# Where TensorE's operands are reordered: VectorE writes them plainly, TensorE reads every fourth column

## The reference

```
x = layer_norm(ALPHA * x + mix, ln1_g, ln1_b)            # (256, 1024)
logits = x @ router_w + router_b;  top 4 of 32 experts, softmax of the four
per expert:  gu   = x[tokens] @ w_gu[e] + b_gu[e]        # 1024 -> 2048
             gate = min(gu[:, :1024], 7);  up = clip(gu[:, 1024:], -7, 7)
             act  = gate * sigmoid(1.702 * gate) * (up + 1)
             y    = act @ w_dn[e] + b_dn[e]              # 1024 -> 1024
out = layer_norm(ALPHA * x + weighted sum of the y's, ln2_g, ln2_b)
```

## Time and profile before

| | us |
|---|---|
| median of three runs | 1175.49 |
| the profiled execution's own time | 1174.48 |
| its span (first to last instruction) | 1172.5 |
| TensorE busy | 1071.5 (91%) |
| VectorE busy | 291.3 (25%) |
| ScalarE busy | 146.0 (12%) |
| DMA queue of the weights | 87.8% of 16 engines' span |

### The profile page before, as it was taken

How to read it: one execution, slowest core, us unless ns; L and a number is a source line. 1 busy time by engine, 2 the same in 40 slices (tenths; PEclk the granted TensorE clock), 3 DMA queues, 4 the chain that set the end, 5 groups by cost and what they waited for, 6 DMA issues and landing times.

```text
span 1172.5 us, 14722 instructions
## 1 busy us (share of the span) xinstructions
PE 1071.5 (91%) x5364; PEld 458.4 (39%) x5365; DVE 291.3 (25%) x770; ACT 146.0 (12%) x313; POOL 29.2 (2%) x54
## 2 busy tenths in 40 slices
PE   7999897888999999998989889999999999999983
PEld 6778544332334333323233323333344333333321
DVE  2354645121212212121212212122212212121114
ACT  2044501010011110000000100001011000000000
POOL 3000400000000000000000000000000000000000
PEclk9999998998999999999999989999999999999997
DMA  9623439764999999999999998999999999999993
GB/s 311 247 110 72 168 137 386 301 241 191 405 427 425 428 427 425 428 427 425 427 427 425 427 427 338 427 425 427 427 425 427 427 426 426 427 426 426 427 420 134
DMA packets 48980, 426.32 MB, mean 364 GB/s; under 512 B 5034, under 2 KB 8923, under 8 KB 16155
## 3 DMA queue, kind: packets, MB, share of 16 engines
q1 hardware_dynamic: 48378, 425.37, 87.8%
q10 hardware_dynamic: 576, 0.61, 0.2%
HBM read 424.91 MB, written 1.05 MB: 363 GB/s over the span
## 4 chain that ended last, share of the span: by engine, by line
PE 62%; DMA 28%; DVE 4%; SPq 3%; issue 2%; ACT 1%; DVEq 0%
PE PB L758 60%; DMA WB<-in_w_gate_up_dram 24%; DMA WB<-in_w_down_dram 3%; SPq L347 2%; ACT S L660 0%; DVE S L1519 0%; DMA X<-in_x_dram 0%; PE PB L1112 0%; DVE K L1502 0%; DVE S L1730 0%; PE PB L765 0%; DVE S L1485 0%; SPq L356 0%; DVE S L1621 0%; DVE S L1622 0%
## 5 line engine op out<-in xcount | busy, mean ns | idle before, releaser
L758 PE MATMUL PB<-WB,S 128*64 128x512 f32 (+5 forms) x3456 | 761.7, 593 | 50.7 <-DMA WB<-in_w_gate_up_dram 25.1
L758 PEld LDWEIGHTS PB<-WB,S 128*64 128x64 f32 (+2 forms) x3456 | 250.8, 139 | 540.5 <-issue 456.2
L1621 DVE TENSOR_SCALAR S<-PB 128x512 f32<-128x512 f32 (+1 forms) x34 | 35.9, 1056 | 652.1 <-PE PB L758 652.1
L758 PE MATMUL PB<-S 32*64 32x512 f32 (+5 forms) x464 | 108.1, 589 | 4.3 <-ACT S L692 1.4
L696 ACT ACTIVATE S<-S 128x512 f32<-128x512 f32 x32 | 20.2, 630 | 552.2 <-DVE S L1621 552.2
L758 PEld LDWEIGHTS PB<-S,X 128*128 128x128 f32 x512 | 61.2, 199 | 13.3 <-issue 12.2
L758 PE MATMUL PB<-S,X 128*128 128x128 f32 x512 | 64.3, 286 | 1.0 <-DVE S L1563 1.0
L758 PE MATMUL PB<-S,WB 128*128 128x256 f32 (+2 forms) x336 | 62.2, 385 | 0.4 <-ACT S L534 0.4
L758 PEld LDWEIGHTS PB<-S 32*64 32x64 f32 (+5 forms) x464 | 34.9, 149 | 65.5 <-issue 54.1
L758 PEld LDWEIGHTS PB<-S,WB 128*128 128x128 f32 (+1 forms) x336 | 48.3, 175 | 12.2 <-issue 2.1
L758 PE MATMUL PB<-WB 128*32 128x128 f32 (+8 forms) x276 | 46.1, 354 | 4.4 <-DVE WB L1450 2.8
(11 more groups left out here) (208 smaller groups left out, 345.1 us busy)
## 6 DMA issues: line engine op xcount, KB each, us to landing
WB<-in_w_gate_up_dram SPq DMA_DIRECT2D x128, 2048.0 KB, 30.4
WB<-in_w_down_dram SPq DMA_DIRECT2D x128, 1024.0 KB, 24.0
WB<-in_w_in_dram SPq DMA_DIRECT2D x3, 2048.0 KB, 15.4
WB<-in_w_in_dram SPq DMA_DIRECT2D x1, 2144.0 KB, 10.5
WB<-in_w_in_dram SPq DMA_DIRECT2D x2, 1024.0 KB, 10.9
WB<-in_w_out_dram SPq DMA_DIRECT2D x2, 1024.0 KB, 10.2
WB<-in_w_out_dram SPq DMA_DIRECT2D x1, 2048.0 KB, 7.8
WB<-in_w_in_dram SPq DMA_DIRECT2D x1, 1040.0 KB, 13.5
```

Of the source, the lines that this page charges most:

```text
L758: return mm_(o, l, r, start=start, stop=stop, skip_group_check=True)
L1621: ts(by_rows(g), in_order(gate), LIMIT, None, ALU.min).then_inc(s[g_ok], 1)
```

## The change

VectorE's three places lose their views and write and read plainly; the helpers `by_rows` and `in_order` are gone. TensorE gets `every_fourth`, which takes columns m, m+4, ... of a half, and uses it in the router's transposes, the gathers and the transposes of the activations. The gather of an extra block writes its PSUM rows in the order that the later steps expect, and reads its moving operand with a step of four columns.

```
+            def every_fourth(a, m):
+                return a.rearrange("p (q m) -> p m q", m=4)[:, m, :]
...
-                                 x_sb[:, b, P * (4 * h + k):P * (4 * h + k) + P], ident)
+                                 every_fourth(x_sb[:, b, 512 * h:512 * h + 512], k), ident)
...
-                        ins = mm(PB[bank][:, P * k:P * k + P], x_sb[:, b, P * (4 * h + k):P * (4 * h + k) + P],
+                        ins = mm(PB[bank][:, P * k:P * k + P], every_fourth(x_sb[:, b, 512 * h:512 * h + 512], k),
                                  oh[:, b, :], k == 0 and b == 0, b == TB - 1)
...
-                    ins = tr(PB[bank][:, P * c:P * c + P], act_sb[:, P * c:P * c + P], ident)
+                    ins = tr(PB[bank][:, P * c:P * c + P], every_fourth(act_sb, c), ident)
...
-                        ins = mm(PB[4][32 * q:32 * q + 32, 0:256], ohx[:, b, :], x_sb[:, b, 256 * q:256 * q + 256],
-                                 b == 0, b == TB - 1)
+                        x_half = x_sb[:, b, 512 * (q // 2):512 * (q // 2) + 512].rearrange("p (s m) -> p m s", m=4)
+                        ins = mm(PB[4][32 * q:32 * q + 32, 0:256].rearrange("p (m s) -> p m s", m=2), ohx[:, b, :],
+                                 x_half[:, 2 * (q % 2):2 * (q % 2) + 2, :], b == 0, b == TB - 1)
...
-                    ins = tr(PB[6][:, 64 * c:64 * c + 64], act_x[0:64, P * c:P * c + P], ident[0:64, 0:64])
+                    ins = tr(PB[6][:, 64 * c:64 * c + 64], every_fourth(act_x[0:64, :], c), ident[0:64, 0:64])
...
-                    yield stt(place(dst[:, b, c]), view(v[:, b, c]), st[:, o + 2:o + 3], view(bt[:, c]), ALU.mult, ALU.add)
+                    yield stt(dst[:, b, c], v[:, b, c], st[:, o + 2:o + 3], bt[:, c], ALU.mult, ALU.add)
...
-                ts(by_rows(g), in_order(gate), LIMIT, None, ALU.min).then_inc(s[g_ok], 1)
-                ts(by_rows(u), in_order(up), LIMIT, -LIMIT, ALU.min, ALU.max).then_inc(s[clip], 1)
+                ts(g, gate, LIMIT, None, ALU.min).then_inc(s[g_ok], 1)
+                ts(u, up, LIMIT, -LIMIT, ALU.min, ALU.max).then_inc(s[clip], 1)
...
-                    ins = stt(in_order(yf[:, b, c]), by_rows(x_sb[:, b, c]), ALPHA, in_order(PB[2 * b + h][:, :]), ALU.mult,
-                              ALU.add)
+                    ins = stt(yf[:, b, c], x_sb[:, b, c], ALPHA, PB[2 * b + h][:, :], ALU.mult, ALU.add)
```

More of the change, by code:

```diff
@@ L1502, in half_stats, with norm @@
                 return dve.bn_stats(st[:, 12 * b + 6 * h:12 * b + 6 * h + 6], v[:, b, 512 * h:512 * h + 512])
[L1504 to L1511, removed]
+            def norm(v, b, n, g, bt, dst, loaded):
                 o = 24 + 4 * b
@@ L1533, in _ @@
                 link(half_stats(y, b, 1))
-                for ins in norm(y, b, b + 1, lng, lnb, x_sb, "ln_ld", by_rows, in_order):
+                for ins in norm(y, b, b + 1, lng, lnb, x_sb, "ln_ld"):
                     ins.then_inc(s["x1ok"], 1)
```

## The result

The changed kernel took 1198.18 us (median of 4 runs, 1194.85 to 1201.06) against 1175.35 for the kernel before: a ratio of 1.0198, interval 1.0181 to 1.0215. I had forecast 1171 in a range up to 1199. It is slower by 23 us, and my forecast had the wrong sign. That 1198 still lies within the range is luck: two errors of price nearly cancel, as the part on the prediction shows.

The account below looks back on a forecast made before the run. TensorE's path to 292.59, its path from about 651 to 711.93, and what follows the last expert set the end, the DMA queue deciding between. 1174.48 - 4.6 (VectorE) with loads at 0 gave 1169.9, against the median 1170.9, said 1171; range 1168.5 to 1199.

Parts of the forecast that it names:

- The three paths: Cost of load growth d, the longest of: queue 80 x d; TensorE to 711.93, 324 x d - 14.1; TensorE throughout, 604 x d - 33.8.
- their spare time: TensorE's slack in pairs at the DMA queue's pace: 5.03 us each, 14.1 in 486:651 plus 19.7 in 879:1110, 33.8 us.
- its second gap: DMA queue standing still at 708 to 712 us, ended by the issue at 711.93; forecast to move to about 708.4.
- I take d = 0 for the forecast: TensorE's gathers and transposes: a weight load with a step of four float32 grows by 0; forecast's chance 0.45.
- the one at 0.33: Gathers and transposes: weight loads pay VectorE's surcharge, 68 to 92 ns each, giving 1179 to 1193 us; chance 0.33.
- the third case: Weight loads pay more than VectorE's surcharge: at 155 ns a load, +55 us, 1231; chance 0.09.
- The surcharge taken over from VectorE: VectorE's price for leaving neighbouring columns, 0.53 ns a column read, 0.72 written, applied to TensorE's loads: 68 and 92 ns.
- The first gather: Gather in 190:197 at the lower clock: 0.21 us an instruction, so it could hide another 0.09 of load growth.
- The extra blocks' moving operand: Extra blocks' gathers, read with the step twice a run: 0 to 0.5 us a block, 1.1 at most, taken as 0.
- VectorE's 4.6 us: Gain from plain access: X writes in the norm 1.4, first expert's clips 0.7, extra blocks' clips 0.7 + 0.7, last sums 1.1.
- the 0.7 of the first expert's clips: First expert's two clips, for which TensorE idles until 215.89: 2 x 0.37 = 0.7 us gained.
- the second case: Weight loads pay VectorE's surcharge, 1179 to 1193 us; chance 0.33, a tenth of it counted as same, the rest slower.

Follow-up runs that it names:

- step 3 run: Changed kernel with the experts' gathers loading every third column instead of every fourth (wrong expert results, good for times alone): 1175.10 us, one run.

## Why the prediction was wrong

- *What bounds the kernel* was read rightly. The three paths and their spare time (33.8 us in all) give the right answer as soon as the right price is put in: 15 gathers at the full clock x 3.89 us = 58.4, less 33.8, is +24.6. The step 3 run, +30 us of TensorE's time for some 2.7 of the kernel's, agrees with the spare time, and so does its second gap.
- *The step that failed* is "I take d = 0 for the forecast", the growth of a gather's weight load. It is 0.240 - 0.115 = 0.125 us. The reasons I gave for 0 (a short step, loads that run ahead) were not read from any row; the row that I did have, 16 loads in 1.87 us, said that a plain load already was as long as the product that hides it, and VectorE's blocked forms had a price of 0.53 to 0.72 ns a column. Of my cases the one at 0.33 came nearest in time, with the right place and sign, but the measured price lies between its 68 to 92 ns and the third case's 155.
- *The surcharge taken over from VectorE* was too small, 68 to 92 ns against 125, and I charged it to the transposes as well, which pay nothing that shows. The two errors nearly cancel: 604 loads x 0.092 = 55.6, and 480 x 0.122 = 58.4 (0.122 being 3.89 / 32). That the measured time lies within the range rests on this, and is luck.
- *The first gather* was read rightly: at the lower clock a plain instruction takes 0.21 us, and a load with a step 0.24, so 0.09 of the growth was hidden as said and the rest, 1.0 us in all, showed.
- *The extra blocks' moving operand* cost 0.92 us each, not 0 to 0.5. That four products share the time held: in the changed kernel's trace the 16 start in groups of four, at 254.97, 255.40, 255.85 and 256.31. The groups are some 0.45 us apart, 0.22 before, so one product grew by 0.23 us and not by 0.14. For an estimate, 256 pieces at the loads' 1.88 ns are 0.48 us, near the 0.45.
- *VectorE's 4.6 us*: the durations came as forecast (the last sum even at 682 ns, so 1.35 us for the four instead of 1.1), but the 0.7 of the first expert's clips was turned into a loss by TensorE's clock, +1.5 at the loop's entry. I had written that no row tells what the shorter wait does to the clock, and taken nothing.
- *The chances* do not add up as written. With a tenth of the second case, "same" is 0.11 + 0.13 + 0.03 = 0.27, not 0.25, and "slower" 0.30 + 0.09 = 0.39, not 0.41. The forecast does not change by it.

The sum with the measured prices: 24.6 + 1.0 + 1.8 - 4.9 + 1.5 = +24.0, against 1197.83 - 1174.48 = +23.35 for the two profiled executions. So close an agreement is partly luck. The sum leaves out the pass of 59.49 (+1.6), and it has 1.4 us for the norm, where the router's transposes start 2.45 us earlier (179.99 against 182.44); the same start lies between 179.6 and 181.6 in the traces of the kernels with the plain write of X.

## What to carry to other kernels

Before a reordering is moved from one engine's writes into another's reads, count how many 16-byte pieces the reader opens, and check whether its loads have cover. A row in which the products are short and the loads full shows it: where the loads alone set the pace, any growth is paid in full. Two float32 columns to a piece were enough here, four apart were not, and laying the weights two rows deep instead of four kept VectorE's plain writes and a gather at 4.04 us. Where two resources run close to one another, work out the spare time first: it makes the cost of a step flat up to a point and steep beyond it.

## What the runs showed that I had not expected

A float32 weight load with a step takes 1.88 ns for each 16 bytes opened where that is longer than the 0.11 us of a plain load; with steps of 4 and 8 it takes the same at either clock (0.24 us, first and second gathers). The same columns as a float32 transpose cost 0.12 to 0.16 us instead of 0.25. A moving operand with the step pays as well: 16 products of 256 columns, four beside one another, in 1.99 instead of 1.07 us. And where a wait was made 0.6 us shorter, TensorE's slow stretch moved onto later work that had nothing to spare, at 1.5 to 2.7 us; in the two kernels with products of zeros in the gap at the loop's entry, the stretch at that place was gone.
